# A four-block network kernel on one core: small attention, recurrence and scan products issued in alternating pairs

## What is computed

```python
s = jnp.einsum('bqhd,bkhd->bhqk', qi, k) * scale + ci[..., None] - c_keys
p = jax.nn.softmax(jnp.where(k_pos[None, :] <= q_pos[:, None], s, -jnp.inf), axis=-1)
return jnp.einsum('bhqk,bkhd->bqhd', p, v)
```

## Time and profile before

| | us |
|---|---|
| median of 3 runs (lowest, highest) | 1678.33 (1677.52, 1679.55) |
| the profiled execution | 1679.45 |
| its span, first to last instruction | 1677.7 |
| PE busy | 1603.7 |
| DVE busy | 1157.2 |
| ACT busy | 793.4 |
| mean granted TensorE clock | 0.987 |

### The profile page before, as it was taken

One profiled execution on the slowest core, in us unless ns is written; L12 is line 12 of the kernel. 1 busy time (PEld: TensorE's weight loads), 2 busy tenths in 40 slices (PEclk: granted clock), 3 DMA queues, 4 the chain that ended last, 5 costly groups with the idle time before them and its releaser, 6 DMA issues.

```text
span 1677.7 us, 23127 instructions
## 1 busy us (share of the span) xinstructions
PE 1603.7 (96%) x9280; PEld 1353.9 (81%) x9280; DVE 1157.2 (69%) x1825; ACT 793.4 (47%) x1079; POOL 58.8 (4%) x72
## 2 busy tenths in 40 slices
PE   8988999998999999999999998999999999899998
PEld 6788876678998888987799887866775678789997
DVE  5787766449986675776687566898863585466653
ACT  4555564444543354545354533656524544444442
POOL 0000000000000000000000003430020000000000
PEclk9988999999999999999999999999999999999999
DMA  9884442324867734433555553422332344245542
GB/s 391 297 322 155 183 191 94 116 105 174 343 236 306 299 148 151 151 126 126 201 201 226 178 197 105 149 90 96 131 110 76 151 151 151 76 151 184 193 176 75
DMA packets 41369, 292.86 MB, mean 175 GB/s; under 512 B 4528, under 2 KB 4784, under 8 KB 6704
## 3 DMA queue, kind: packets, MB, share of 16 engines
q1 hardware_dynamic: 40112, 284.04, 45.6%
q10 hardware_dynamic: 1152, 7.34, 1.1%
HBM read 288.22 MB, written 3.15 MB: 174 GB/s over the span
## 4 chain that ended last, share of the span: by engine, by line
PE 74%; DVE 16%; ACT 5%; issue 3%; DMA 2%; POOL 1%; DVEq 0%; ACTq 0%; SPq 0%; POOLq 0%
PE ps L1032 32%; PE ps L1040 27%; DVE ring_at_lo L1221 5%; ACT w_hi L1210 2%; DMA ring_at<-stream 2%; DVE arena_at L1135 1%; PE ps L2932 1%; PE ps L2471 1%; DVE arena_at L2050 1%; PE ps L999 1%; PE ps L3142 1%; PE ps L1976 1%; PE ps L2229 1%; PE ps L2919 1%; PE ps L2202 1%
## 5 line engine op out<-in xcount | busy, mean ns | idle before, releaser
L1221 DVE TENSOR_TENSOR ring_at_lo<-ring_at,w_hi 128x2048 fp32r<-128x2048 f32 (+1 forms) x218 | 495.2, 2274 | 202.5 <-ACT w_hi L1210 202.3
L1210 ACT ACTIVATE w_hi<-ring_at 128x2048 fp32r<-128x2048 f32 (+1 forms) x218 | 414.3, 1903 | 222.4 <-PE ps L1032 132.9
L1040 PE MATMUL ps<-h_hi,w_hi 128*128 128x256 f32 x1440 | 414.3, 288 | 3.7 <-DVE hT_at_lo L1485 2.5
L1040 PE MATMUL ps<-h_hi,ring_at_lo 128*128 128x256 f32 x1440 | 415.2, 288 | 0.0
L1040 PE MATMUL ps<-hT_at_lo,w_hi 128*128 128x256 f32 x1440 | 410.3, 285 | 0.0
L1032 PE MATMUL ps<-w_hi,arena_at_lo 128*128 128x512 f32 x1232 | 390.5, 398 | 2.8 <-DVEq L4277 0.8
L1040 PEld LDWEIGHTS ps<-h_hi,w_hi 128*128 128x128 f32 x1440 | 278.0, 193 | 14.9 <-issue 14.4
L1032 PEld LDWEIGHTS ps<-w_hi,arena_at_lo 128*128 128x128 f32 x1232 | 229.4, 189 | 58.8 <-issue 6.9
L1040 PEld LDWEIGHTS ps<-h_hi,ring_at_lo 128*128 128x128 f32 x1440 | 276.4, 192 | 0.0
L1040 PEld LDWEIGHTS ps<-hT_at_lo,w_hi 128*128 128x128 f32 x1440 | 274.0, 190 | 0.3
L1032 PE MATMUL ps<-ring_at_lo,arena_at_lo 128*128 128x512 f32 x616 | 244.1, 396 | 0.0
(11 more groups left out here) (457 smaller groups left out, 1685.9 us busy)
## 6 DMA issues: line engine op xcount, KB each, us to landing
ring_at<-stream SPq DMA_DIRECT2D x266, 1024.0 KB, 4.9
arena_at<-bias ACTq DMA_DIRECT2D x4, 768.0 KB, 6.0
kept<-arena_at ACTq DMA_DIRECT2D x2, 1024.0 KB, 10.7
arena_at<-kept ACTq DMA_DIRECT2D x2, 1024.0 KB, 7.5
arena_at<-mem SPq DMA_DIRECT2D x1, 1024.0 KB, 7.3
x_res<-x SPq DMA_DIRECT2D x1, 1024.0 KB, 17.1
out<-x_res SPq DMA_DIRECT2D x2, 512.0 KB, 2.8
con<-consts SPq DMA_DIRECT2D x1, 640.0 KB, 23.1
```

What stands on the lines that cost most here:

```text
L1040: mm = pe.matmul(k.ps[:, bank + q // 2, (q % 2) * TOK:(q % 2 + 1) * TOK], w[:, q * P:(q + 1) * P], x, start=first and n == 0 and q % 2 == ...
L1210: act.activation(k.w_hi[:, s % HI, 0:n, :], k.ring[:, c % RING, 0:n, :], ACT.Identity).then_inc(k.hi_done, 1)
L1221: dve.tensor_tensor(k.w_lo[:, c % RING, 0:n, :], k.ring[:, c % RING, 0:n, :], k.w_hi[:, s % HI, 0:n, :].bitcast(F32), ALU.subtract).then_i ...
```

## The change

In the four small stages the products of two neighbours (heads h and h+1, or scan steps i and i+1) are issued together, alternating between the two: first product of the even one, first product of the odd one, second of the even, second of the odd, and so on. The even and the odd one use different parts of the array. `scores`, `drive` come in even steps, `values`, `out` in odd ones, at the place of the odd partner; waits are those of the odd partner. S5's h and b2 get a third buffer. The paces of `in2`'s guests change. Neighbours' and Ssd's paces don't. Fox is changed as Neighbours is, but its mask and forget-gate products of both heads run first, head by head.

```diff
 Ssd.tensor
-        def out(h):
-            pe.wait_ge(*m["weights_in"].at(h + 1))
-            if h >= 2 and h % 2 == 0:
-                pe.wait_ge(*m["head_taken"].at(h // 2))
...
+        def out(p):
+            pe.wait_ge(*m["weights_in"].at(2 * p + 2))
+            if p >= 1:
+                pe.wait_ge(*m["head_taken"].at(p))
...
             for s in range(2):
+                for h in (2 * p, 2 * p + 1):
+                    rows = slice(HP * (h % 2), HP * (h % 2) + HP)
+                    mm = pe.matmul(k.ps[rows, 6, 0:TOK], self.xt[:, s, h * HP:(h + 1) * HP],
+                                   self.e[:, h % 3, s * TOK:(s + 1) * TOK], start=s == 0, stop=s == 1)
+                    if s == 1:
+                        mm.then_inc(m["head_out"].sem, 1)
...
             args(h, 1)
-            if h >= 1:
-                out(h - 1)
+            if h >= 2 and h % 2 == 0:
+                out(h // 2 - 1)
 Neighbours.tensor
         def scores(h):
             if h >= 2:
-                pe.wait_ge(*m["maxima_in"].at(h - 1))
+                pe.wait_ge(*m["maxima_in"].at(h))
             for t in range(TT):
+                for g in (h, h + 1):
+                    mm = pe.matmul(k.ps[:, 4 + g % 2, t * TOK:(t + 1) * TOK], self.q(g, t), self.keys(g),
+                                   start=True, stop=True)
...
         def values(h):
-            pe.wait_ge(*m["probs_taken"].at(h + 1))
+            pe.wait_ge(*m["probs_taken"].at(h + 2))
...
         for h in range(NH + 3):
-            if h < NH:
+            if h < NH and h % 2 == 0:
                 scores(h)
             if 1 <= h <= NH:
                 turn(h - 1)
-            if 2 <= h <= NH + 1:
-                values(h - 2)
+            if 3 <= h <= NH + 1 and h % 2:
+                values(h - 3)
 S5.tensor
             if i >= 2:
-                pe.wait_ge(*m["s5_turned_in"].at(2 * i - 2))
+                pe.wait_ge(*m["s5_turned_in"].at(2 * i))
...
-            pe.wait_ge(*m["s5_turned_out"].at(2 * i + 2))
+            pe.wait_ge(*m["s5_turned_out"].at(2 * i + 4))
...
         for i in range(S5T + 3):
-            if i < S5T:
+            if i < S5T and i % 2 == 0:
                 drive(i)
-            if 2 <= i < S5T + 2:
-                out(i - 2)
+            if 3 <= i < S5T + 2 and i % 2:
+                out(i - 3)
 S5.vector, turn_out
-            if i >= 2:
-                dve.wait_ge(*m["s5_used"].at(i - 1))
+            if i >= 3:
+                dve.wait_ge(*m["s5_used"].at(i - 2))
 Fox.tensor
             if h >= 2:
-                pe.wait_ge(*m["probs_in"].at(h - 1))
+                pe.wait_ge(*m["probs_in"].at(h))
 block2_stages
-        Woven(k, in2, (Threaded(gate), paced([(0, 3, 8, 14)])), (Threaded(s5_stage), paced([(0, 21, 12, 60)])),
-              (Threaded(hg_prep), paced([(0, 1, 49, 50), (1, 3, 50, 58)])),
-              (Threaded(hgrn), paced([(0, 21, 60, 88)])),
-              (Threaded(prep), paced([(0, 6, 88, 96)])),
-              (Threaded(fox), paced([(0, 11, 96, 116)], True))),
+        Woven(k, in2, (Threaded(gate), paced([(0, 3, 8, 14)])), (Threaded(s5_stage), paced([(0, 21, 12, 70)])),
+              (Threaded(hg_prep), paced([(0, 1, 56, 57), (1, 3, 57, 66)])),
+              (Threaded(hgrn), paced([(0, 21, 70, 94)])),
+              (Threaded(prep), paced([(0, 6, 94, 100)])),
+              (Threaded(fox), paced([(0, 11, 100, 116)], True))),
```

More of the change, by code:

```diff
@@ L2226, in values @@
                 pe.wait_ge(k.dve_took, k.dve_groups[self.norm.first + 10 + h // 8])
-            rows = slice(HP * (h % 2), HP * (h % 2) + HP)
             for s in range(2):
-                mm = pe.matmul(k.ps[rows, ADA, 0:TOK], self.v(h, s), self.pt[:, h % 2, s, :], start=s == 0, stop=s == 1)
-            mm.then_inc(m["heads_out"].sem, 1)
+                for g in (h, h + 1):
+                    rows = slice(HP * (g % 2), HP * (g % 2) + HP)
+                    mm = pe.matmul(k.ps[rows, ADA, 0:TOK], self.v(g, s), self.pt[:, g % 2, s, :], start=s == 0,
+                                   stop=s == 1)
+                    if s == 1:
+                        mm.then_inc(m["heads_out"].sem, 1)
         pe.wait_ge(k.act_took, k.act_groups[self.norm.first + 7])
@@ L3366, in scores @@
             if h >= 2:
[L3367 to L3377 removed]
+                pe.wait_ge(*m["probs_in"].at(h))
+            for g in (h, h + 1):
+                bank = k.ps[:, 4 + g % 2, :]
+                pe.matmul(bank, k.mask_bf[:, 10 * P:11 * P], k.mask_bf[:, 6 * P:10 * P], start=True, stop=False,
+                          skip_group_check=True)
+                pe.matmul(bank, k.con("ident")[0:32, g:g + 1].broadcast_to([32, P]),
+                          self.negc[0:32, :].unsqueeze(1).broadcast_to([32, 2, TOK]), start=False, stop=False,
+                          skip_group_check=True)
+            for t in range(TT):
+                for g in (h, h + 1):
+                    rows = slice(64 * (g % 2), 64 * (g % 2) + 64)
+                    mm = pe.matmul(k.ps[:, 4 + g % 2, t * TOK:(t + 1) * TOK],
+                                   self.qkT[rows, g // 2, t * P:(t + 1) * P], self.qkT[rows, 4 + g // 2, :],
+                                   start=False, stop=True, skip_group_check=True)
+                    if t == TT - 1:
+                        mm.then_inc(m["scores_in"].sem, 1)
         def turn(h):
@@ L3389, in values @@
         def values(h):
-            pe.wait_ge(*m["probs_taken"].at(h + 1))
-            if h >= 2 and h % 2 == 0:
+            pe.wait_ge(*m["probs_taken"].at(h + 2))
+            if h >= 2:
                 pe.wait_ge(*m["heads_hi"].at(h // 2))
                 pe.wait_ge(*m["heads_lo"].at(h // 2))
-            rows = slice(64 * (h % 2), 64 * (h % 2) + 64)
             for s in range(2):
-                mm = pe.matmul(k.ps[rows, 7, 0:TOK], self.v[:, s, h * 64:(h + 1) * 64], self.pt[:, h % 2, s, :],
-                               start=s == 0, stop=s == 1)
-            mm.then_inc(m["heads_out"].sem, 1)
+                for g in (h, h + 1):
+                    rows = slice(64 * (g % 2), 64 * (g % 2) + 64)
+                    mm = pe.matmul(k.ps[rows, 7, 0:TOK], self.v[:, s, g * 64:(g + 1) * 64], self.pt[:, g % 2, s, :],
+                                   start=s == 0, stop=s == 1)
+                    if s == 1:
+                        mm.then_inc(m["heads_out"].sem, 1)
         pe.wait_ge(*self.prep.m["fox_qk"].at(4))
@@ L3404, in tensor @@
         for h in range(FOXH + 3):
-            if h < FOXH:
+            if h < FOXH and h % 2 == 0:
                 scores(h)
@@ L3408, in tensor @@
                 turn(h - 1)
-            if 2 <= h <= FOXH + 1:
-                values(h - 2)
+            if 3 <= h <= FOXH + 1 and h % 2:
+                values(h - 3)
             yield
@@ L3999, in block2_stages @@
     ab = s5w.take(2, 2, 512)
-    g, h, b2 = s5w.take(1, 512)[:, 0, :], s5w.take(2, 512), s5w.take(2, 512)
-    assert gla.at <= at_gl + 6 * D
+    g, h, b2 = s5w.take(1, 512)[:, 0, :], s5w.take(3, 512), s5w.take(3, 512)
+    assert gla.at <= at_gl + 6 * D and s5w.at <= SPARE
     hw = region(k, work)
```

44 lines of the change are left out of this document (22 added, 22 removed).

## The result

The changed kernel takes 1652.59 us (median of 4 runs, 1651.83 to 1653.66) where the kernel before takes 1678.94 on the same chip: a ratio of 0.9838 with a 95% interval of 0.9816 to 0.986, 26 us off, where 11 were forecast. That is just inside the low end of the forecast's whole range (1652). The profiled execution took 1653.26, with a span of 1651.5.

A forecast was written before the change was run, and what follows sets the result against it. PE, busy 96% of the span, was taken as the bound, with DVE close to full in S5. Terms -7.1-12.0+2.4+3.5+1.4+0.6 = -11.2 us gave 1667 us; own range 1659 to 1675, whole range 1652 to 1696.

The forecast's parts named there:

- rival 3: Whole kernel: overlap, and DVE hides more; S5 at DVE's own 13.1 per pair, half the other new waits go: 1652, chance 0.13.
- So every change costs 0.165: PE, all four small stages: each change of array shape costs 0.165 us; fewer changes take 12.5 us off PE.
- 5 slots instead of 8: Overlap within a pair of four two-pass products, a slot being 0.219 us; S5's `out` 9 instead of 16; 38.6 us off PE.
- rival 2: Only row pairs (scores, drive) overlap, values and `out` take all their slots: +15, 1693 us, chance 0.07.
- S5, +2.4: S5 stage: 8 x 0.3 us slower; all 20 us off PE come back as waits at L2932.
- 14.2 per pair: S5's loop of drive, DVE and out, two steps: 7.6 plus 6.6 us; without it DVE alone needs 13.1, PE 11.4.
- 13.9 per pair: S5 before the change, at the same main work: a step takes 6.95 us, so 13.9 for two.
- HGRN, +3.5: HGRN stage: 19.4 main steps instead of 22.7 give 4.5 us less cover; bounds 0 and 4.5, taken nearer the upper.
- Neighbours, -12.0: Neighbours stage: 15.8 us saved, less 1.0 at the first turn and waits of 1.1 at heads 6 and 12, 0.6 at 14.
- Fox, +0.6: Fox stage, 16 main steps instead of 20: gain 4 x (0.5+1.31) = 7.2, against waits of 9.1 less the 1.3 of before.
- prep, +1.4: Prep stage: POOL's chain as long, one main step less beside it, PE already waiting 1.17 at its end: 1.4 us slower.
- Rival 1: No overlap, only shape changes saved: S5's loop 16.2 against 13.9 (+18), Fox +6, in all +25, 1703 us; chance 0.22.

## Why the prediction was wrong, point by point

- **Direction and mechanism right, size wrong.** Faster, 26 us instead of 11, at rival 3's number (1652). Rival 3's condition, S5 at DVE's own pace and half of the other waits gone, is not what happened: S5's turns took 14.0, not 13.1, and Neighbours' waits were longer than forecast, not shorter. That its number came out is luck.
- **"So every change costs 0.165"**: Ssd has 2 changes and 4 slots less per pair, 1.21 us; times 8, 9.7, less two waits that are new (0.8 at L1963, 0.7 at L1977) is 8.2, where 7.6 are measured. Right within 0.6.
- **"5 slots instead of 8"**: it is 4 (timeline of Ssd), and 8 instead of 9 in `out`. The step that failed is "a's second pass must follow its first on the same part, b's first can run beside it, and so on", which lets b run a slot behind a; in fact both start together. That is 1 more slot per pair in Ssd and 2 in the other three: 8 + 16 + 16 + 8 = 48 slots, 10.5 us more off PE (61.5 instead of 51). The Trainium skill ("TensorE: Matmul & The Clock Gate", Part 3) has tiles start about 4 ns apart; the trace has 7 and 13 ns, of the same order and somewhat more. Its other sentence, that weight loads overlap only when the row group differs, the trace does not bear out: in the Ssd pair above, whose two parts both read all 128 rows, the loads at 190.400 and 190.407 begin while the first two matmuls (190.132 to 190.568) are under way. And that column pairs would save no slot was the prediction's own conclusion from that sentence; L1976's 17.2 us down to 8.7 refute it, and rival 2 with it.
- **S5, +2.4, measured -9.3: the step that cost most.** The sum has 8 x 14.2 and 19.2 for the other 13.8 main steps, 132.8, and 126.2 are measured; for before it has 130.4 with 13.9 per pair, and 135.5 are measured at the same main steps. So 6.6 of the 11.7 us are the kernel after and 5.1 the kernel before. After: the step that failed is "Together **14.2 per pair**" taken for all eight pairs. `drive` starts at 1044.4, 1054.3, 1069.4, 1082.3, 1098.9, 1111.2, 1122.0 and 1138.2. From the second to the last that is (1138.2-1054.3)/6 = 14.0 per pair, so the loop is there and its size is nearly right (1.3 us in six turns). But it has six turns, not eight: the first distance, with no `out` in it, is 9.9, and in the 28.0 us from the last `drive` on PE is busy for 27.6. The rest, 5.3, lies at these two ends. In the 14.0 lies also a mean clock of 0.92, which the sum did not have; with `drive` behind `out` the same distance is 12.9 ((1128.2-1050.7)/6), at DVE's own pace, forecast as 13.1. Before: "13.9 per pair" counts work alone, and before S5 also held waits (2.4) and a clock of 0.98; the new paces took 3.3 of that back by themselves. As for the signs: L2943 waits 12.1, not 20; DVE is 94% busy, as said.
- **HGRN, +3.5, measured -3.0.** "4.5 us less cover" became nothing: with and without the pairs L3142's waits fell at the new paces, and a clock drop went. I took the bound near the upper end for the row's 5.2 us of waits, and did not ask why they were there: by the windows PE ran at half clock behind one of them, which a shift of the guests can move. That the shift can gain as well as lose was missing from the bounds.
- **Neighbours, -12.0, measured -9.3.** L2217 waits 10.2, against 2.6 before. At heads 6, 12 and 14, which the forecast names, it waits 1.21, 1.24 and 0.76, 3.2 in all against the 2.8 forecast. What the sum put at nothing are heads 7, 9 and 11: 1.48, 1.51 and 1.47, where before it was 0.43 each, 3.2 more. The first turn, whose loss of 1.0 the forecast had, waits 1.2 longer (2.51). Gain with complete overlap: 15.8 + 3.5 (8 x 2 slots) = 19.3, less 7.6 of new waits is 11.7. Behind the first turn the clock is 0.72 from 262 to 268, another 1.7; 0.7 stays open.
- **Fox, +0.6, measured -1.3; prep, +1.4, measured +0.7.** Close in size, Fox's sign aside. Fox's waits are 6.4 at the turns (forecast 7.7), of which 3.7 at head 4 (forecast 4.5), and 0.6 at the scores (forecast 1.4). The clock loss behind head 4's, 1.7, was not in the sum, nor the 8 slots more that complete overlap gives; they nearly cancel.
- **Clock.** No term of the sum had it. It costs some 6 us more than before over the span, 3.1 of which in the cross attention, where nothing changed.
- **Rival 1** was told apart by its condition, but its price of S5 (+18) is off by 19: without overlap it was 1.3 faster than before.

In sum, of the 15 us between forecast and result by the table, S5 is 11.7, HGRN 6.5, Fox 1.9, prep 0.7 and Ssd 0.5, against 3.1 in the cross attention, 2.7 in Neighbours and 1.4 ahead of Ssd.

## What to carry to other kernels

Small products of two independent heads or steps whose operands and results lie in different rows or columns of the array are worth placing next to each other: each pair takes the time of one, in float32 as well. Alternating is not needed as long as no more than three records of the one stand ahead of the other's first. Once PE is cheaper, look at every loop between PE and the engine that it feeds: launching a step's first product right behind the last use took another 6 us out of S5, at no work. A new wait of PE of 2 to 4 us may cost another 1 to 3 us of slow clock behind it, though the length of the wait alone doesn't tell (below); and paces are to be compared by a run, since ten more main steps for S5 gained here and four more lost.

## What the runs showed of the hardware

- At full clock, records in disjoint parts of the array start 7 to 13 ns apart, also when three records of the other part stand between them in the program. With eight ahead the overlap begins beside the fifth.
- Column parts of which both read all 128 rows overlap as fully as row parts: 8.7 against 17.2 us for L1976's 64 records.
- Behind the changed kernel's five waits of 2.5 to 3.7 us in the small stages the clock was at the lower level for some us (main products 0.43 apart instead of 0.23), at once or up to about 1 us later. The wait's length alone doesn't decide it. Behind one and the same wait at the end of the second input product, 3.24 us before and 3.25 after, the windows of the two kernels have 0.58 and 1.00:

```profile
1328.00:1335.00 7.00, 6.70 (x36) 6.73 (x37) 3.05 (x3) 6.97 (x19) 0.00 (x0) 0.58 0.87 369
```

```profile
1300.00:1307.00 7.00, 7.00 (x54) 6.78 (x55) 3.66 (x6) 6.97 (x18) 0.00 (x0) 1.00 0.89 363
```

- The clock can also fall late. In the version with `drive` behind `out`, sixteen records behind a wait of 2.33 us run in 1.92, at full clock, and the main products slow down 5 us later, behind a second, shorter wait (timeline and window):

```profile
1101.76 1.92 PE L2943 MATMUL ps<-arena_at 128*32 128x256 f32 x16 [2.33 <-DVE arena_at L3048]
...
1107.15 0.63 PE L1032 MATMUL ps<-w_hi,h_hi 128*128 128x512 f32 x1
```

```profile
1105.00:1112.00 7.00, 6.84 (x26) 5.28 (x27) 7.00 (x14) 2.58 (x6) 0.00 (x0) 0.76 0.00 0
```

- An unchanged stretch of 43.9 us took 3.0 or 4.8 more in some versions, with the clock alone to show for it: a difference of 3 us between two versions can be that.
